# The second layer's FFN input as seven block products in place of eight

## The reference, cut to what matters

```python
D_MODEL = 1024; SEQ = 512; CTX_LEN = 256; DEPTH = 2; D_FF = 2816

def swiglu(h, w_in, w_out):          # h: 512 x 1024, w_in: 1024 x 5632, w_out: 2816 x 1024
    g, u = jnp.split(h @ w_in, 2, axis=-1)
    return (jax.nn.silu(g) * u) @ w_out
...
    f = swiglu(rms_norm(xl, g_ffn_pre[i]) * (1 + sc2) + sh2, w_ffn_in[i], w_ffn_out[i])
    xl = xl + gt2 * rms_norm(f, g_ffn_post[i])
```

## Time and profile before

| | |
|---|---|
| median of three timed runs | 1669.67 us |
| profiled execution, span from first to last instruction | 1668.4 us |
| its own time with what lies around the span | not printed; the median of the timed runs is 1.3 us above the span |
| TensorE busy | 1632.3 us, 98% |
| VectorE, ScalarE, GpSimd busy | 752.8, 653.9, 652.4 us |
| granted TensorE clock, mean | 0.997 |

### The profile page before, as it was taken

The page is one execution under the profiler, slowest core; times in us unless marked ns, Lnnn a source line. Parts: engine busy times, 40 slices in busy tenths (PEclk is TensorE's granted clock), DMA queues, the critical chain, the costliest instruction groups (busy, mean ns, idle before and its releaser), DMA issues.

```text
span 1668.4 us, 25361 instructions
## 1 busy us (share of the span) xinstructions
PE 1632.3 (98%) x9966; PEld 1364.7 (82%) x9966; DVE 752.8 (45%) x1149; ACT 653.9 (39%) x1169; POOL 652.4 (39%) x400
## 2 busy tenths in 40 slices
PE   6999999999999999999999999999999999999998
PEld 4878887788887887879999888888887888888886
DVE  5846557725698644404655430027863341011103
ACT  4352136726332122223555342237864423123222
POOL 2312222036555444544642044234433354444442
PEclk9999999999999999999999999999999999999999
DMA  9742201023566655534656637324012443333332
GB/s 357 259 139 77 47 19 52 2 76 101 180 199 208 209 162 177 167 95 123 175 167 194 194 102 158 86 74 127 27 52 76 140 139 99 107 96 99 92 101 76
DMA packets 212613, 209.83 MB, mean 126 GB/s; under 512 B 16312, under 2 KB 180752, under 8 KB 212112
## 3 DMA queue, kind: packets, MB, share of 16 engines
q1 hardware_dynamic: 198488, 162.39, 32.8%
q10 hardware_dynamic: 14008, 45.83, 8.7%
HBM read 202.39 MB, written 4.23 MB: 124 GB/s over the span
## 4 chain that ended last, share of the span: by engine, by line
PE 89%; DVE 3%; ACT 3%; issue 2%; POOL 1%; DMA 1%; SPq 0%; DVEq 0%; ACTq 0%; POOLq 0%
PE ps L2010 46%; PE ps L2057 26%; PE ps L2377 3%; PE ps L2320 3%; PE ps L2283 3%; PE ps L2240 2%; PE ps L2166 1%; POOL w_lo L584 1%; PE ps L2261 1%; PE ps L2127 1%; PE ps L2039 1%; DVE prob L1490 1%; DMA mod_early<-in_w_mod 1%; ACT w_hi L921 1%; ACT junk L911 1%
## 5 line engine op out<-in xcount | busy, mean ns | idle before, releaser
L584 POOL TENSOR_TENSOR w_lo<-w_raw,w_hi 128x1024 fp32r<-128x1024 f32 (+1 forms) x211 | 537.3, 2549 | 829.2 <-ACT w_hi L921 829.2
L2010 PE MATMUL ps<-h_hi,w_hi 128*128 128x512 f32 (+1 forms) x1488 | 496.7, 352 | 3.4 <-POOL w_lo L584 2.4
L2010 PE MATMUL ps<-h_hi,w_lo 128*128 128x512 f32 (+1 forms) x1488 | 492.4, 349 | 0.0
L2010 PE MATMUL ps<-h_lo,w_hi 128*128 128x512 f32 (+1 forms) x1488 | 491.3, 349 | 0.0
L921 ACT ACTIVATE w_hi<-w_raw 128x1024 fp32r<-128x1024 f32 (+1 forms) x267 | 280.5, 1051 | 303.2 <-PE ps L2057 258.3
L2010 PEld LDWEIGHTS ps<-h_hi,w_hi 128*128 128x128 f32 x1488 | 270.6, 190 | 45.7 <-issue 8.1
L2010 PEld LDWEIGHTS ps<-h_hi,w_lo 128*128 128x128 f32 x1488 | 270.2, 190 | 36.3
L2010 PEld LDWEIGHTS ps<-h_lo,w_hi 128*128 128x128 f32 x1488 | 270.1, 190 | 35.9
L1460 DVE TENSOR_TENSOR hid_f<-silu_g,ps 128x512 f32<-128x512 f32 (+1 forms) x66 | 39.3, 595 | 252.7 <-PE ps L2010 252.3
L584 DVE TENSOR_TENSOR w_lo<-w_raw,w_hi 128x1024 fp32r<-128x1024 f32 x53 | 70.3, 1328 | 139.3 <-ACT w_hi L921 139.3
L2057 PE MATMUL ps<-w_hi,hid_hi 128*128 128x512 f32 x428 | 132.3, 390 | 0.5 <-ACT mod_row L933 0.5
(11 more groups left out here) (278 smaller groups left out, 2003.5 us busy)
## 6 DMA issues: line engine op xcount, KB each, us to landing
w_raw<-in_w_ffn_in SPq DMA_DIRECT2D x132, 512.0 KB, 3.9
w_raw<-in_w_ffn_out SPq DMA_DIRECT2D x66, 512.0 KB, 3.6
mod_raw<-in_w_mod ACTq DMA_DIRECT2D x42, 512.0 KB, 4.7
mod_early<-in_w_mod SPq DMA_DIRECT2D x30, 512.0 KB, 10.4
w_raw<-in_na_w_in SPq DMA_DIRECT2D x29, 512.0 KB, 3.8
full<-in_w_mod ACTq DMA_DIRECT2D x15, 512.0 KB, 5.6
w_raw<-in_ab_w_in SPq DMA_DIRECT2D x18, 256.0 KB, 7.7
w_raw<-in_ab_w_in SPq DMA_DIRECT2D x9, 512.0 KB, 4.6
```

The costliest lines, as they stand in the source:

```text
L584: eng.tensor_tensor(w_lo[:, u % RING, 0:width], w_raw[:, u % RAW, 0:width], w_hi[:, u % RING, 0:width].bitcast(F32), ALU.subtract).then_in ...
L2010: mm = pe.matmul(o[0], sta(x, o), mov(y, o), start=first and n == 0, stop=last and n == 2)
```

## The change

The product h @ w_in of the second layer is cut into blocks of two by two: the 512 tokens into two halves of 256, the 1024 features into two halves of 512, and of the weights, for each column block j, gate and up. Eight block products are replaced by seven (Winograd's form of Strassen's scheme), from sums of blocks of both operands:

- Token sums, once: T1 to T4 in `hs` (VectorE, `hc_sums`), then seven operands of 4 x 256 columns in high and low parts (`hc_hi` by ScalarE, `hc_lo` by VectorE and GpSimd).
- Weight sums, for each block j: s1 = a21 + a22, s3 = a11 - a21, s2 = s1 - a11, s4 = a12 - s2 in `w_sum` (GpSimd, one buffer for each part), of 128x512 each. Their high parts and that of a22 come from ScalarE (`high_jobs`), the low parts from VectorE (`low_jobs`; for block 0 four of five from GpSimd). They lie in a ring of eight (`FAST = 8`). The gate unit still has its full `w_hi` and `w_lo`, in the old ring; the up unit has none.
- TensorE (`fast_product`) takes for each block the products 5, 7, 2, 1, 3, 4, 6, each 4 x 3 matmuls of 256 columns, four banks of PSUM for one block and four for the next. Products 3, 4 and 6 are added onto products 5, 7 and 1 in the same bank, once those have been copied or summed by ScalarE and VectorE.
- Seven VectorE operations of 256 columns join the products to gate and up and multiply them (`combine`).
- All 22 blocks run in one stage. The hidden block, 128 x 512, goes to DRAM (`hid_far`) over SP's queue, comes back in the output stage in three buffers, and is split there.
- The output stage takes all 22 units of rows at once; `take_half`, `add_half` and `end_add` of this layer are gone, and the last norm reads PSUM.
- The late modulation rows are added one per block, in blocks 2 to 9.

```diff
+        def weight_sum(eng, j, part):
+            if j:
+                eng.wait_ge(s_hi_done, NT + job(j - 1, part) + 1)
+                eng.wait_ge(*job_low_ready(job(j - 1, part)))
...
+            eng.tensor_tensor(out(part), x, y, op).then_inc(w_summed, 1)
+        def raw_free(eng, v):
+            if v not in ups:
+                eng.wait_ge(w_hi_done, ring_no[v] + 1)
+                eng.wait_ge(*low_ready(v))
+            if sp("fi1") <= v < sp("fo1L"):
+                eng.wait_ge(w_summed, NT + 4 * j + 4)
+            if v in ups:
+                eng.wait_ge(s_hi_done, NT + job(j, "a22") + 1)
+                eng.wait_ge(*job_low_ready(job(j, "a22")))
# SP
+                if u in ups and u >= sp("fi1") + 7:
+                    hid_store((u - sp("fi1")) // 2 - 3)
+                if sp("fo1L") < u <= sp("fo1L") + 3:
+                    hid_store(FT - 4 + u - sp("fo1L"))
# GpSimd
+            weight_sum(pool, 0, "s1")
+            weight_sum(pool, 0, "s3")
             pre("ffn1L", 3)
-            feed(sp(("fi1L", 0)) + 1)
-            feed(sp(("fo1L", 1)) + FH - 1)
+            weight_sum(pool, 0, "s2")
+            weight_sum(pool, 0, "s4")
+            feed(sp("fi1") + 2)
+            low_jobs(job(0, "s3"))
+            for x, p in HC_LOW_POOL[:3]:
+                hc_low(pool, x, p)
+            low_jobs(job(0, "s4"))
+            for x, p in HC_LOW_POOL[3:]:
+                hc_low(pool, x, p)
+            low_jobs(job(0, "s2"))
+            for j in range(FT):
+                if j + 1 < FT:
+                    for part in ("s1", "s3", "s2", "s4"):
+                        weight_sum(pool, j + 1, part)
+                feed(sp("fi1") + 2 * (j + 2))
+            feed(sp("fo1L") + FT - 1)
# ScalarE, one block
+                    act.wait_ge(s_used, NT + job(j, "s1") + 1)
+                    act.activation(part_p[:], ps(fast_banks(j)[2], 0, HALF1), ACT.Copy).then_inc(fp_copied, 1)
+                    if j + 1 < FT:
+                        high_jobs(job(j + 1, "s3"))
+                    act.wait_ge(fp_2, NT + j + 1)
+                    act.wait_ge(f_t, NT + j + 1)
+                    act.activation(part_p[:], ps(fast_banks(j)[1], 0, HALF1), ACT.Copy).then_inc(fp_copied, 1)
+                    feed(s + 2 * (j + 2) if j + 2 < FT else sp("fo1L") + j + 2 - FT)
+                    act.wait_ge(f_11, NT + j + 1)
+                    act.activation(sum_11[:], sum_11[:], ACT.Silu).then_inc(f_silu1, 1)
+                    high_jobs(job(j + 1, "s2") if j + 1 < FT else HID_JOB + 2)
# VectorE
+            def combine(j):
+                dve.wait_ge(f_u, NT + j + 1)
+                dve.tensor_tensor(sum_12[:], ps(d, 0, HALF1), sum_u[:], ALU.add).then_inc(f_12, 1)
+                if j:
+                    dve.wait_ge(hid_out, 16 * j)
+                dve.tensor_tensor(first, ps(f, 0, HALF1), sum_u[:], ALU.add).then_inc(f_21, 1)
+                dve.tensor_tensor(second, sum_u[:], sum_t[:], ALU.add).then_inc(f_22, 1)
...
+                dve.tensor_tensor(first, first, sum_11[:], ALU.mult)
...
+                dve.tensor_tensor(second, second, sum_12[:], ALU.mult).then_inc(hid_made, 1)
+            for j in range(FT + 1):
+                if j:
+                    combine(j - 1)
...
+                if j + 1 < FT:
+                    low_jobs(job(j + 1, "s1"))
+                dve.wait_ge(s_used, NT + job(j, "s3") + 1)
+                dve.wait_ge(fp_copied, NT + 2 * j + 1)
+                dve.tensor_tensor(sum_t[:], ps(f, 0, HALF1), part_p[:], ALU.add).then_inc(f_t, 1)
+                if j + 1 < FT:
+                    low_jobs(job(j + 1, "s3"))
+                dve.wait_ge(w_used, ring_no[sp("fi1") + 2 * j + 1])
+                dve.wait_ge(fp_copied, NT + 2 * j + 2)
+                dve.tensor_tensor(sum_11[:], ps(a_, 0, HALF1), part_p[:], ALU.add).then_inc(f_11, 1)
+                low_jobs(job(j + 1, "s2") if j + 1 < FT else HID_JOB + 2)
+                add_rows(("fi1", j))
# TensorE
+                    pe.wait_ge(*{3: (fp_copied, NT + 2 * j + 1), 4: (f_t, NT + j + 1), 6: (f_11, NT + j + 1)}[p])
+                for k in range(4):
+                    for x, y in (("hi", "hi"), ("hi", "lo"), ("lo", "hi")):
+                        mm = pe.matmul(ps(bank, 0, HALF1), w[x][:, k * P:(k + 1) * P], hc[y][:, p - 1, k, :],
...
+            fast_product(0, 2)
+            norm_turn(3)
+            for j, p in ((0, 1), (1, 2), (1, 1)):
+                fast_product(j, p)
+            for j in range(FT):
+                for p in (5, 7, 2, 1, 3, 4, 6):
+                    if p > 2 or j > 1:
+                        fast_product(j, p)
```

More of the change, by code:

```diff
@@ L50 @@
 UNIT = 1024
+FAST = 8
+HALF1 = SEQ // 2
+FAST_JOBS = ("s1", "s3", "s4", "a22", "s2")
 VR = AKV + 2 * RANK
@@ L151, in weight_units @@
     rows("out1L", a["na_w_out"][0], range(KT))
-    for half in range(2):
-        ffn_in(("fi1L", half), 1, range(FH * half, FH * half + FH))
-        rows(("fo1L", half), a["w_ffn_out"][1], range(FH * half, FH * half + FH))
+    ffn_in("fi1", 1, range(FT))
+    rows("fo1L", a["w_ffn_out"][1], range(FT))
     return units, start
@@ L264, in build @@
     by_dve[sp("v0")] = True
-    by_dve[sp(("fo1L", 1)) + FH - 1] = True
+    by_dve[sp("fo1L") + FT - 1] = True
     by_dve[sp("out1L") + KT - 1] = True
-    by_dve[sp(("fi1L", 0)) + 1] = True
-    low_no = [sum(x == by_dve[u] for x in by_dve[:u]) for u in range(n_units)]
+    ups = range(sp("fi1") + 1, sp("fi1") + 2 * FT, 2)
+    ring_no = [sum(x not in ups for x in range(u)) for u in range(n_units + 1)]
+    low_no = [sum(by_dve[x] == by_dve[u] and x not in ups for x in range(u)) for u in range(n_units)]
+    jobs = [(j, part) for j in range(FT) for part in FAST_JOBS] + [(k, "hid") for k in range(FT)]
+    job_dve = [j > 0 or part in ("a22", "hid") for j, part in jobs]
+    job_no = [sum(x == job_dve[q] for x in job_dve[:q]) for q in range(len(jobs))]
+    HID_JOB = len(FAST_JOBS) * FT
     with ExitStack() as ctx:
@@ L376, in build @@
             bias_m = sb("bias_m", [P, 6 * P], scope=s1)
+        with ExitStack() as s1:
+            with ExitStack() as s2:
+                hs = sb("hs", [P, 2, 7, 4, HALF1], scope=s2)
+            hc_hi = sb("hc_hi", [P, 7, 4, HALF1], F32R, scope=s1)
+            hc_lo = sb("hc_lo", [P, 7, 4, HALF1], F32R, scope=s1)
+            w_sum = sb("w_sum", [P, 4, UNIT // 2], scope=s1)
+            part_p, sum_11, sum_t, sum_u = (sb(n, [P, HALF1], scope=s1) for n in ("part_p", "sum_11", "sum_t", "sum_u"))
+        hs_hi, hs_lo = hs[:, 0], hs[:, 1]
         prob0_t = [x.rearrange("p a n -> p (a n)")[:, 0:10 * P].rearrange("p (x n) -> p x n", x=2)
@@ new lines, in job_free, with job_source @@
+        def job_free(eng, q):
+            if q < FAST:
+                eng.wait_ge(w_used, ring_no[sp("fi1")])
+                return
+            k, part = jobs[q - FAST]
+            if part == "hid":
+                eng.wait_ge(w_used, ring_no[sp("fo1L") + k + 1])
+            else:
+                eng.wait_ge(s_used, NT + q - FAST + 1)
+        def job_source(q):
+            j, part = jobs[q]
+            if part == "hid":
+                return hid_raw[:, j % 3, :]
+            if part == "a22":
+                return w_raw[:, (sp("fi1") + 2 * j + 1) % RAW, UNIT // 2:]
+            return w_sum[:, ("s1", "s3", "s4", "s2").index(part), :]
@@ new lines, in _ @@
+            low_jobs(job(0, "a22"))
+            for j in range(FT + 1):
+                if j:
+                    combine(j - 1)
+                if j == 13:
+                    modulation(11)
+                if j == FT:
+                    break
+                a_, _, _, f = fast_banks(j)
+                if j + 1 < FT:
[10 more added lines that the diff above has]
+                add_rows(("fi1", j))
```

438 lines of the change are left out of this document (324 added, 114 removed).

## The result

The changed kernel takes 1722.3 us in the median (1721.7 to 1723.7), the kernel before 1669.5 us beside it: a ratio of 1.0314, 95% interval 1.0299 to 1.0329. It is slower by 52.8 us, where 47 had been predicted, inside the range of 1684 to 1750. The span of the profiled execution is 1721.9 us, its mean granted clock 0.989.

A forecast was written before the change was run, and what follows sets the result against it. TensorE, busy 98%, bounded the kernel before; turn-taking at the SBUF port would bound the new loop. Input stage 1329 + 21 x 12.1 - 2 + 8.7 = 1590, 49 later; end -1.4; span 1716, median 1717, range 1684 to 1750 us.

The forecast's parts named there:

- TensorE's saving: Input-stage column blocks: 84 matmuls of 120.5 ns take 10.12 us instead of 10.88, saving 16.7 us if nothing else is late.
- The port: SBUF access: VectorE operations with both inputs in SBUF exclude GpSimd's, less 0.15 us overlap at each change of hands.
- The circle: Input-stage loop: waits through GpSimd, VectorE and ScalarE queues close at 12.1 us per block; 11.4 to 12.7 given chance 0.60.
- whole lengths: Rival for the input loop: full turns without overlap, 13.5 us per block, 1748 us in all; chance 0.07.
- Rows: Blocks 2 to 9: each modulation-row accumulation on VectorE adds 1.09 us behind GpSimd, 8.7 us together.
- The start: Beginning of the input stage: GpSimd's long queue and port turns make block 0 end at 1329 us (bounds 1317 and 1333).
- the rival with the free port: Input loop: port no bound, TensorE sets 10.12 us per block, three modulation steps cost 1.8; 1663 us; chance 0.12.
- The end: After the last matmul: without adding two halves, about 6.1 us instead of 7.5, a gain of 1.4.
- The sum: Whole kernel: input stage ends at 1590, 49 us later; end gains 1.4; span 1716, median 1717 us.
- the gapless port (10.4): Rival for the input loop: port filled without gaps, 10.4 us per block, 1683 us; chance 0.14.
- The half clock: Rival for TensorE in the loop's gaps: 0.21 us per matmul, 17.9 us per block, 1843 us in all; chance 0.05.
- The break-even of 10.2 us per block: Input loop: the change is faster only if blocks take less than 10.2 us, with TensorE setting the pace.

The follow-up runs named there:

- One input: Changed kernel with VectorE's low parts of weight sums and a22 (blocks 1 to 21) reading one SBUF input, by a reduction without the subtraction: 1684.5 us.
- Three edits of the queues: Separate edits of the changed kernel: ScalarE's w_hi copy earlier, 1729.8 us; VectorE's sum_t before low s1, 1710.5; weight sums moved from GpSimd to VectorE, 1687.4.
- the four versions at about 10.1 in most blocks: With weight sums on VectorE: queues reordered, 1680.3 us; plus start rewritten, 1672.5; plus root, modulation-sum and clock-filling edits, 1664.0; the last without clock filling, 1665.6.

## Why the prediction was right, step by step

- *TensorE's saving.* 84 matmuls in 10.12 us were predicted, 10.08 are measured wherever nothing else was late: 120.0 ns each.
- *The port.* Right: operations on two SBUF inputs and GpSimd's exclude each other, those with one in PSUM don't. One input shows the cause, and not only the place. The rule isn't the whole of it: the scaling of a tile, with one SBUF input, waited too (1.75 for 0.75, above).
- *The circle.* 12.1 predicted, 12.28 to 12.32 measured, and step by step the same: 2.48 for 2.44, 0.55 for 0.54, 1.15 and 1.19 for 1.135, 1.40 for 1.335, 0.34 for 0.42. The 0.2 is spread over the steps. The overlap of 0.15 at a change of hands is there too: whole lengths would have given 13.5. Three edits of the queues moved the time by +7.5, -11.8 and -34.9 us where the same layout had +6, -13 and -35; the first met waits for loads that the layout did not have.
- *Rows.* 1.09 each predicted, 0.91 measured.
- *The start.* 2.8 us too early (block 0 at 1329, measured 1333.4 less a shift of 1.5 and the mark's 0.1). The shift is in the trace before anything changes: the output product of the attention starts at 1243.20, not 1241.72. Of the 2.8, some 0.9 lie ahead of product 4 and some 1.9 in products 4 and 6: the 3.2 us for them took TensorE's full pace, but behind a wait of 7.33 us they ran at a granted clock of 0.50, with 0.21 us from start to start, and took 5.1. The prediction had the lower clock come only after block 0, where it would cost nothing. (First matmul of product 4; stage, columns as in the earlier trace rows.)

```profile
1328.19 0.58 PE L2977 MATMUL ps<-hc_hi,s_hi 128*128 128x256 f32 x1 [7.33 <-DVE sum_t L2287]
...
1328.00:1332.00 4.00, 3.81 (x18) 3.81 (x19) 1.97 (x4) 3.75 (x6) 3.83 (x3) 0.50 0.02 6
```

- *The products of the modulation.* Priced at 0.6 each, and only in the rival with the free port: the sum of the forecast has no term for them, and gives no reason. The second cost more:

```profile
1494.12 0.58 PE L2977 MATMUL ps<-hc_hi,w_hi 128*128 128x256 f32 x1 [5.13 <-DVE mod_col L1698]
...
1495.00:1500.00 5.00, 5.00 (x25) 5.00 (x25) 1.16 (x3) 1.33 (x2) 1.50 (x1) 0.50 0.52 150
```

  It uses bank 3, which product 2 of the same block needs, and VectorE reads it only behind combine(12). Block 13 takes 18.24 us, 5.9 more than an ordinary one: 5.13 of waiting, and behind it TensorE at the lower clock, 27 matmuls in 5.9 us in place of 3.2. The next three run at 10.08, 11.52 and 11.49, which gives 3.8 back: some 2 us in all.
- *The end.* 5.6 us after the last matmul (1716.3 to 1721.9), 6.1 predicted, 7.5 before.
- *The sum.* Input stage 1596.6 against 1590: shift 1.5, start 2.8, loop with rows and modulation 2.4. That the loop is so close is in part luck: 0.2 more in each block and the modulation's 2 made it longer, the rows and the short blocks 1 and 2 (11.18 and 11.78 us) made it shorter. End 0.5 less. Span 1721.9 against 1716, the median 1722.3 against 1717. The profiled execution is the slowest of the four, 1723.7 us, 1.8 above its span; the others have spans of 1719.9 to 1720.7, also 1.8 below their times. The 1.3 of the prediction set the median of three runs against the span of one.

Of the rivals, the gapless port (10.4) did not come: sum s2 waits for low s2, and everything for one copy, as had been held against it. The half clock came only in block 13, behind the 5.13 us. Elsewhere in the loop, with gaps of 1.2 and 1.4 us in a block with a row, up to 1.7 in one without, and one of 2.12, the granted clock stayed at 1.00 (1345 to 1490 and 1505 to 1596 us). The break-even of 10.2 us per block holds as a rule of thumb: the four versions at about 10.1 in most blocks ended between 0.6% slower and 0.3% faster, by their start and by the products of the modulation. That eight products with the result by way of DRAM would do better still wasn't tried.

## What to carry to other kernels

When two engines exclude each other, their busy shares say little: lay the queues out in written order with the rows' lengths, find the circle, and try an edit in that layout before it is made. The layout was good to 2 us for single edits of the loop; it was 8 and 10 us off where the start and the modulation's products came in, and a number that agrees doesn't show its circle: look for waits that the layout lacks. Work on the slower side of the pair was better given to the faster engine here, even to the busiest one: 0.69 us for 1.285, and changes of hands less. And a saving in the engine that is the bound is not had until the start of the stage is as short as before: here the way from a span of 1721.9 to one of 1662.1 us was some 48 us of loop and 12 of start. Price TensorE's work behind a long wait at the lower clock: here that was 1.9 us at the start and 2.7 in block 13.

## What was not expected of the hardware

- GpSimd can wait for a whole row of VectorE operations, not for one: 3.59 us for an operation of 0.19, 6.68 for one of 1.285. In the loop of the changed kernel it got in behind every single one. In the loop VectorE's first operation had itself been waiting for GpSimd; in the row none had. Whether that decides it isn't settled. By the Trainium skill (SBUF — State Buffer, "Who interferes with whom"), whoever issues first has the port; at 1305.99 GpSimd's operation began 0.07 us ahead of VectorE's next one on two SBUF inputs and still came last. These are recorded starts; when either asked for the port, the trace doesn't show.
- One SBUF input doesn't always keep VectorE clear of GpSimd: the reduction of 512 columns kept its 0.676 us, the scaling of 1024 columns took 1.75 in place of 0.74 (at 1300.03 above, and at 1294.24 in the changed kernel).
- Filling a gap of TensorE raised the granted clock from 0.64 to 1.00 in that stretch (1310 to 1315 us) and gained nothing that could be measured, since VectorE was the next to be late.
